# Last feed-forward of a two-layer trunk: rounded activations and their remainder as one 512-column moving operand

## The chip, the cores and the metric

One core of one Trainium2 chip runs the whole program. The metric is the device time of one execution in microseconds (us). The engines are TensorE (PE in the profile, with its weight loads as PEld), VectorE (DVE), ScalarE (ACT), GpSimd (POOL) and SyncE (SP), which here only issues loads and stores.

## The reference, cut to what matters

The trunk has two layers over 272 tokens (16 meta tokens and 256 real ones), width 1024, feed-forward width 2816. Each layer adds a feed-forward, a mixer and a second feed-forward to the residual stream. At the end a last RMSNorm is applied and the meta tokens are dropped, so the second feed-forward of the last layer is needed for the 256 real tokens alone.

```python
def swiglu(x, w_gu, w_down):
    a, b = jnp.split(x @ w_gu, 2, axis=-1)
    return (jax.nn.silu(a) * b) @ w_down

for l in range(DEPTH):
    h = h + 0.5 * swiglu(rmsnorm(h, ffn1_norm[l]), ffn1_w_gu[l], ffn1_w_down[l])
    h = h + mixer(...)
    h = h + 0.5 * swiglu(rmsnorm(h, ffn2_norm[l]), ffn2_w_gu[l], ffn2_w_down[l])
h = rmsnorm(h, final_norm)
return h[:, CHUNK:]
```

Everything is float32.

## The kernel before

Activations lie with features on the partitions and tokens along the free axis. Every product of a weight block W (128x128) with an activation block X is made in the rounded format fp32r, in which both operands are split into a rounded part and a remainder: W = w_hi + w_lo and X = xh + xl. Three matmuls add into the same PSUM bank: w_hi with xh (L706), w_hi with xl (L707) and w_lo with xh (L708). Each has its own weight load, also where two of them in a row have the same weights. `use` issues this for the 8 blocks of a "piece" of weights (128x1024), 24 matmuls in all, and then raises `piece_done`.

The weights come as a stream of pieces through a ring of four slots. For each piece SP loads `raw`; ACT rounds it to `w_hi` (`split_hi`, L274) once the piece three before the one to come has been used, and DVE forms `w_lo = raw - w_hi` (`split_lo`, L437), which raises `lo_ready`. That frees the `raw` slot and lets TensorE use the piece.

A feed-forward has 66 pieces. The first 44 are 11 iterations of four: two pieces for two gate chunks (banks 0 and 1), two for two up chunks (banks 2 and 3). In iteration `it` DVE's queue holds, in this order: the split of ring slot 0; L491, which waits for the second gate piece and writes `scl = gate * r` (r is the norm's factor per token) and so raises `gate_scaled`; the splits of slots 1 and 2; L497, which waits for the second up piece and ACT's silu and writes `gv = up * act` and so raises `up_gated`; the split of slot 3; L500 (`gv = gv * r`); L502, which waits for ACT's rounded copy `gh` (L317) and writes `gl = gv - gh`. ACT's queue holds: the rounding of slots 0 and 1, silu (L315, waits for `gate_scaled`), the rounding of slots 2 and 3, and `gh` (L317, waits for L500). Both engines work their queues strictly in this order. TensorE waits for `gate_scaled` of the iteration before ahead of a new gate, and for `up_gated` of the iteration before ahead of a new up.

The other 22 pieces are the down projection, 11 for output chunks 0 to 3 (banks 0 to 3) and 11 for chunks 4 to 7 (banks 4 to 7). Its first piece waits for the last `gate_scaled`, and its fifth block (it goes to banks 2 and 3) for the last `up_gated`. The last two pieces of each eleven close two banks each, and `update_h` (L464) adds half of them to the residual `h`. In the last feed-forward it is followed by ACT's squares for the last norm (L289) and by DVE's multiplication with the gain (L470). After the last piece TensorE sums the squares (L720 to L726), and DVE, ACT and POOL scale `h` for the stores.

In the last layer only the tokens 16 to 271 are worked on, so a matmul of the last feed-forward has 256 columns; those of the first layer have 272.

Of the kernel before, what the change touches and what calls it, by code (L numbers as in the profile page):

```python
# [25 lines left out]
F32R = mybir.dt.float32r  # L26
ALU = mybir.AluOpType
ACT = mybir.ActivationFunctionType

P = 128  # L30
# [15 lines left out]
RING = 4  # L46
# [33 lines left out]
def trunk(nc, stream, h_in, gains, gn_gains, tables, squares, h_out):  # L80
    with ExitStack() as ctx:
# [48 lines left out]
        sp = sqh[:, :, :].rearrange("p a t -> p (a t)")[:, 0:SCORES]  # L130
        sp_hi, sp_lo = (g[:, FC - 2:FC, :].rearrange("p a t -> p (a t)")[:, 0:SCORES] for g in (gh, gl))
        pa = xg[:, 0, :, :].rearrange("p a t -> p (a t)")[:, 0:SCORES]
# [16 lines left out]
        def pair(n, q0):  # L149

            return bank[:, n:n + 2, q0:T]

        def first_query(l):
# [29 lines left out]
        gate_scaled, gate_act, up_gated = sem("gate_scaled"), sem("gate_act"), sem("up_gated")  # L183
        g_val, gh_ready, g_ready = sem("g_val"), sem("gh_ready"), sem("g_ready")

        unit_evicted, swapped, rot_cos, rot_sin, rotated = sem("unit_evicted"), sem("swapped"), sem("rot_cos"), sem("rot_sin"), sem("rotated")
# [246 lines left out]
        def _(eng):  # L433
# [27 lines left out]
            def update_h(rnd, p, b, factor, q0, final=False):  # L461

                c = 2 * p
                eng.scalar_tensor_tensor(h[:, c:c + 2, q0:T], pair(b, q0), factor, h[:, c:c + 2, q0:T],  # L464
                                         ALU.mult, ALU.add).then_inc(h_new, 1)
                if final:

                    eng.wait_ge(sq_ready, rnd * PAIRS + (p + 1))
                    for k in (c, c + 1):
                        eng.tensor_scalar(h[:, k, q0:T], h[:, k, q0:T], gain[:, rnd, k:k + 1], None,  # L470
                                          ALU.mult).then_inc(scaled_out, 1)
                else:
                    eng.wait_ge(h_new, (rnd - 1) * PAIRS + (p + 1))
                    scale_h(rnd, p, q0)
                    lo_of_h(rnd, p, q0)

            def ffn(l, f):
# [6 lines left out]
                with eng.Fori(0, ITERS) as it:  # L484
                    i = fi * ITERS + it
                    for j in range(4):
                        if j == 1:

                            eng.wait_ge(r_ready, l * 3 + 2 * f + 1)
                            eng.wait_ge(piece_done, base + it * 4 + 2)  # L490
                            eng.tensor_tensor(scl[:, :, q0:T], pair(0, q0), twice(r, q0), ALU.mult).then_inc(gate_scaled, 1)  # L491
                        if j == 3:

                            eng.wait_ge(gate_act, i + 1)
                            eng.wait_ge(g_ready, i + 1)
                            eng.wait_ge(piece_done, base + it * 4 + 4)
                            eng.tensor_tensor(gv[:, :, q0:T], pair(2, q0), act[:, :, q0:T], ALU.mult).then_inc(up_gated, 1)  # L497
                        split_lo(base + it * 4 + (j + RING), (off + j) % RING)
# [197 lines left out]
        def _(pe):  # L696
            def use(n, slot, blocks, before=None):
# [11 lines left out]
                mm.then_inc(piece_done, 1)  # L709

            def k_half(src_h, src_l, half, b, q0, halves=2, c0=0):
# [27 lines left out]
            def ffn(l, f):  # L739
                fi = l * 2 + f  # L740
                off = 0 if f == 0 else FFN + MIX
                base = l * PER_LAYER + off
                q0 = first_query(l) if f else 0

                def gate(n, half, before=None):
                    use(n, (off + half) % RING, k_half(xh, xl, half, 0, q0), before)

                def up(n, half, before=None):
                    use(n, (off + 2 + half) % RING, k_half(xh, xl, half, 2, q0), before)

# [4 lines left out]
                with pe.Fori(1, ITERS) as it:  # L755
                    pe.wait_ge(gate_scaled, fi * ITERS + it)
                    gate(base + it * 4, 0)
                    gate(base + it * 4 + 1, 1)
                    pe.wait_ge(up_gated, fi * ITERS + it)
                    up(base + it * 4 + 2, 0)  # L760
                    up(base + it * 4 + 3, 1)
                pe.wait_ge(gate_scaled, fi * ITERS + ITERS)
                for q in range(QUADS):
                    for c in range(ITERS):
# [9 lines left out]
                        use(base + s, (off + s) % RING,  # L774
                            [(gh[:, k, q0:T], gl[:, k, q0:T], bank[:, 4 * q + m, q0:T], first, last)
                             for k, m, first, last in blocks],

                            {4: lambda: pe.wait_ge(up_gated, fi * ITERS + ITERS)} if q == c == 0 else None)

# [240 lines left out]
```

## Time and profile before

| | |
|---|---|
| time, median of 3 runs | 1347.0 us (1346.66 to 1347.02) |
| span of the profiled execution, first to last instruction | 1345.0 us |
| granted TensorE clock, mean over the span | 0.997 |
| TensorE busy | 1321.6 us (98%), 10440 matmuls |
| DVE busy | 845.6 us (63%) |
| ACT busy | 640.3 us (48%) |
| POOL busy | 36.2 us (3%) |
| the last feed-forward | from about 1145 us of the span to about 1333 us |

The profile shows one execution, known by its span; what lies around the span, 2.0 us, is in the runs' times and not in the trace. Times in the rows count from the first instruction. A matmul's duration in the rows holds its way through the array, so matmuls overlap in them: the rate is read from the distance between starts.

### The profile page before, as it was taken

How to read it: one execution, taken by the hardware profiler on the slowest of the kernel's cores; microseconds unless marked ns; L12 is line 12 of the kernel's file. 1: busy time of each engine (PE TensorE's matmuls, PEld its weight loads, DVE VectorE, ACT ScalarE, POOL GpSimd, SP SyncE). 2: the span in 40 equal slices, each digit the busy share in tenths (PEclk: the TensorE clock that was granted, in tenths of full speed). 3: DMA queues.
4: the chain of work that ended last, by engine and by line, in shares of the span. 5: the costliest groups of instructions: out<-in, count | busy, mean ns of one | idle time of the engine just before them, and what ended most of it. 6: DMA issues, size and time to landing. Idle time of an engine off the chain costs nothing.

```text
span 1345.0 us, 26386 instructions
## 1 busy us (share of the span) xinstructions
PE 1321.6 (98%) x10440; PEld 1295.3 (96%) x10440; DVE 845.6 (63%) x980; ACT 640.3 (48%) x812; POOL 36.2 (3%) x27
## 2 busy tenths in 40 slices
PE   6999999999999999999999999999999999999996
PEld 6999999999999999999999999999999999999996
DVE  6666557756654776665576665577556557766654
ACT  5444445444545544444444444464545455544441
POOL 1000001000000010000010000010000000100000
PEclk9999999999999999999999999999999999999998
DMA  7655555553334556556556555556543345566651
GB/s 271 193 173 175 180 176 152 178 171 116 106 110 112 169 153 193 175 174 181 174 157 187 173 175 175 180 152 179 171 126 103 117 129 177 184 186 187 185 190 61
DMA packets 61205, 219.53 MB, mean 163 GB/s; under 512 B 6992, under 2 KB 8272, under 8 KB 61008
## 3 DMA queue, kind: packets, MB, share of 16 engines
q1 hardware_dynamic: 60704, 217.93, 53.4%
q8 instruction: 55, 0.90, 0.3%
q10 hardware_dynamic: 432, 0.59, 0.1%
q14 instruction: 14, 0.11, 0.0%
HBM read 217.44 MB, written 1.05 MB: 162 GB/s over the span
## 4 chain that ended last, share of the span: by engine, by line
PE 92%; DVE 4%; issue 2%; ACT 1%; DMA 0%; POOL 0%; DVEq 0%; ACTq 0%; POOLq 0%
PE bank L706 29%; PE bank L707 28%; PE bank L708 28%; PE bank L908 1%; PE bank L894 1%; PE bank L922 1%; PE bank L873 1%; DVE w_lo L437 1%; PE bank L802 1%; ACT act L346 1%; PE bank L785 1%; DVE act L533 0%; DVE r L459 0%; DMA gain<-gains 0%; DVE xg L445 0%
## 5 line engine op out<-in xcount | busy, mean ns | idle before, releaser
L437 DVE TENSOR_TENSOR w_lo<-raw,w_hi 128x1024 fp32r<-128x1024 f32 x408 | 507.7, 1249 | 308.2 <-ACT w_hi L274 304.2
L706 PE MATMUL bank<-xh,w_hi 128*128 128x272 f32 (+1 forms) x2240 | 646.6, 289 | 11.7 <-DVE xl L451 11.2
L274 ACT ACTIVATE w_hi<-raw 128x1024 fp32r<-128x1024 f32 x408 | 427.9, 1056 | 457.5 <-PE bank L708 454.2
L707 PE MATMUL bank<-xl,w_hi 128*128 128x272 f32 (+1 forms) x2240 | 642.7, 287 | 0.0
L708 PE MATMUL bank<-xh,w_lo 128*128 128x272 f32 (+1 forms) x2240 | 640.5, 286 | 0.0
L706 PEld LDWEIGHTS bank<-xh,w_hi 128*128 128x128 f32 x2240 | 423.3, 189 | 14.1 <-DVE xl L451 10.5
L707 PEld LDWEIGHTS bank<-xl,w_hi 128*128 128x128 f32 x2240 | 421.9, 188 | 0.2
L708 PEld LDWEIGHTS bank<-xh,w_lo 128*128 128x128 f32 x2240 | 422.0, 188 | 0.0
L706 PE MATMUL bank<-gh,w_hi 128*128 128x272 f32 (+1 forms) x1024 | 293.1, 286 | 0.0
L707 PE MATMUL bank<-gl,w_hi 128*128 128x272 f32 (+1 forms) x1024 | 292.1, 285 | 0.0
L708 PE MATMUL bank<-gh,w_lo 128*128 128x272 f32 (+1 forms) x1024 | 291.9, 285 | 0.0
L708 PEld LDWEIGHTS bank<-gh,w_lo 128*128 128x128 f32 x1024 | 193.0, 188 | 0.0
L707 PEld LDWEIGHTS bank<-gl,w_hi 128*128 128x128 f32 x1024 | 192.9, 188 | 0.0
L706 PEld LDWEIGHTS bank<-gh,w_hi 128*128 128x128 f32 x1024 | 192.6, 188 | 0.1
L317 ACT ACTIVATE gh<-gv 128x544 f32 (+1 forms) x44 | 28.7, 653 | 92.4 <-DVE gv L500 92.4
L250 POOL TENSOR_TENSOR ssq<-ssq,sqh 128x544 f32<-128x544 f32 x20 | 33.7, 1685 | 1297.7 <-ACT sqh L289 1297.7
L502 DVE TENSOR_TENSOR gl<-gv,gh 128x544 f32 (+1 forms) x44 | 31.6, 717 | 42.3 <-ACT gh L317 42.3
L497 DVE TENSOR_TENSOR gv<-bank,act 128x544 f32<-128x544 f32 (+1 forms) x44 | 31.4, 715 | 23.2 <-PE bank L708 23.2
L280 ACT ACTIVATE xh<-xg 128x544 fp32r<-128x544 f32 (+1 forms) x24 | 15.7, 654 | 59.3 <-DVE xg L445 59.2
L491 DVE TENSOR_TENSOR scl<-bank,r 128x544 f32<-128x544 f32 (+1 forms) x44 | 31.4, 713 | 1.1
L315 ACT ACTIVATE act<-scl 128x544 f32<-128x544 f32 (+1 forms) x44 | 28.1, 638 | 7.8 <-DVE scl L491 7.8
L500 DVE TENSOR_TENSOR gv<-gv,r 128x544 f32<-128x544 f32 (+1 forms) x44 | 31.2, 710 | 0.0
(104 smaller groups left out, 622.3 us busy)
## 6 DMA issues: line engine op xcount, KB each, us to landing
raw<-stream SPq DMA_DIRECT2D x408, 512.0 KB, 3.7
table<-tables SPq DMA_DIRECT2D x1, 2000.0 KB, 9.2
out<-h SPq DMA_DIRECT2D x4, 256.0 KB, 2.7
h<-tokens ACTq DMA_DIRECT2D x2, 272.0 KB, 5.9
h<-tokens SPq DMA_DIRECT2D x2, 272.0 KB, 6.0
dec<-squares SPq DMA_DIRECT2D x1, 192.0 KB, 8.0
square<-squares SPq DMA_DIRECT2D x1, 128.0 KB, 7.9
gain<-gains ACTq DMA_DIRECT2D x1, 28.0 KB, 5.3
```

Source lines behind the costliest of these rows:

```text
L250: pool.tensor_tensor(ssq[:, :, :], ssq[:, :, :], sqh[:, :, :], ALU.add).then_inc(ssq_added, 1)
L274: eng.activation(w_hi[:, slot, :], raw[:, slot, :], ACT.Copy).then_inc(hi_ready, 1)
L315: eng.activation(act[:, :, q0:T], scl[:, :, q0:T], ACT.Silu).then_inc(gate_act, 1)
L317: eng.activation(gh[:, bass.ds(it * 2, 2), q0:T], gv[:, :, q0:T], ACT.Copy).then_inc(gh_ready, 1)
L437: eng.tensor_tensor(w_lo[:, slot, :], raw[:, slot, :], w_hi[:, slot, :].bitcast(F32), ALU.subtract).then_inc(lo_ready, 1)
L491: eng.tensor_tensor(scl[:, :, q0:T], pair(0, q0), twice(r, q0), ALU.mult).then_inc(gate_scaled, 1)
L497: eng.tensor_tensor(gv[:, :, q0:T], pair(2, q0), act[:, :, q0:T], ALU.mult).then_inc(up_gated, 1)
L500: eng.tensor_tensor(gv[:, :, q0:T], gv[:, :, q0:T], twice(r, q0), ALU.mult).then_inc(g_val, 1)
L502: eng.tensor_tensor(gl[:, bass.ds(it * 2, 2), q0:T], gv[:, :, q0:T], gh[:, bass.ds(it * 2, 2), q0:T].bitcast(F32), ALU.subtract).then_inc( ...
L706: pe.matmul(out, wh, hi, start=first, stop=False)
L707: pe.matmul(out, wh, lo, start=False, stop=False)
L708: mm = pe.matmul(out, wl, hi, start=False, stop=last)
```

## The change

In the last feed-forward alone, the rounded activations and their remainders are laid side by side in one tile (`x_both`, `g_both`), so that one matmul with 512 moving columns takes both past the same w_hi: columns 0 to 255 of a bank then hold the product with the rounded part and columns 256 to 511 that with the remainder. The product of w_lo with the rounded part goes to columns 0 to 255, as a matmul of 256 columns. A block has two matmuls and two weight loads in place of three and three. The two halves of a bank have to be added: for gate and up by a `tensor_reduce` over pairs 256 apart, ahead of the multiplication that was there, and for the down projection by a second `scalar_tensor_tensor` on `h`. TensorE now waits for the reduce, not for the multiplication behind it, before it reuses the banks. The other feed-forwards and the mixers keep their instructions.

```diff
-        xh = sb("xh", [P, DC, T], F32R)
-        xl = sb("xl", [P, DC, T], F32R)
-        gh = sb("gh", [P, FC, T], F32R)
-        gl = sb("gl", [P, FC, T], F32R)
+        x_both = sb("x_both", [P, DC, 2, T], F32R)
+        g_both = sb("g_both", [P, FC, 2, T], F32R)
+        xh, xl = x_both[:, :, 0, :], x_both[:, :, 1, :]
+        gh, gl = g_both[:, :, 0, :], g_both[:, :, 1, :]
...
+        def sums(n):
+            return bank[:, n:n + 2, 0:SEQ], bank[:, n:n + 2, SEQ:2 * SEQ]
+        def halves_of(n):
+            return bank[:, n:n + 2, :].rearrange("p b (i t) -> p b t i", i=2)
...
                 # update_h
+                if final:
+                    eng.scalar_tensor_tensor(h[:, c:c + 2, q0:T], sums(b)[0], factor, h[:, c:c + 2, q0:T],
+                                             ALU.mult, ALU.add).then_inc(out_added, 1)
+                    eng.wait_ge(out_added, p + 1)
+                    eng.scalar_tensor_tensor(h[:, c:c + 2, q0:T], sums(b)[1], factor, h[:, c:c + 2, q0:T],
+                                             ALU.mult, ALU.add).then_inc(h_new, 1)
...
                             # DVE, gate
+                            if last:
+                                eng.tensor_reduce(scl[:, :, q0:T], halves_of(0), mybir.AxisListType.X, ALU.add).then_inc(gate_summed, 1)
+                                eng.wait_ge(gate_summed, it + 1)
+                                eng.tensor_tensor(scl[:, :, q0:T], scl[:, :, q0:T], twice(r, q0), ALU.mult).then_inc(gate_scaled, 1)
...
                             # DVE, up
+                            if last:
+                                eng.tensor_reduce(gv[:, :, q0:T], halves_of(2), mybir.AxisListType.X, ALU.add).then_inc(up_summed, 1)
+                                eng.wait_ge(up_summed, it + 1)
+                                eng.tensor_tensor(gv[:, :, q0:T], gv[:, :, q0:T], act[:, :, q0:T], ALU.mult).then_inc(up_gated, 1)
...
+            def use_wide(n, slot, blocks, before=None):
+                pe.wait_ge(lo_ready, n + 1)
+                for b, (both, bk, first, last) in enumerate(blocks):
+                    if before and b in before:
+                        before[b]()
+                    wh = w_hi[:, slot, b * P:(b + 1) * P]
+                    wl = w_lo[:, slot, b * P:(b + 1) * P]
+                    pe.matmul(bank[:, bk, 0:2 * SEQ], wh, both, start=first, stop=False, skip_group_check=True)
+                    mm = pe.matmul(bank[:, bk, 0:SEQ], wl, both[:, 0, :], start=False, stop=last, skip_group_check=True)
+                mm.then_inc(piece_done, 1)
...
+                last_ffn = first_query(l) > 0 and f == 1
+                gate_free, up_free, freed = (gate_summed, up_summed, 0) if last_ffn else (gate_scaled, up_gated, fi * ITERS)
...
-                    pe.wait_ge(gate_scaled, fi * ITERS + it)
+                    pe.wait_ge(gate_free, freed + it)
...
-                    pe.wait_ge(up_gated, fi * ITERS + it)
+                    pe.wait_ge(up_free, freed + it)
...
-                pe.wait_ge(gate_scaled, fi * ITERS + ITERS)
+                pe.wait_ge(gate_free, freed + ITERS)
...
+                        before = {4: lambda: pe.wait_ge(up_free, freed + ITERS)} if q == c == 0 else None
```

## Rows read from the trace of the kernel before

**Rows 1.** Page, part 1: busy time and share of the span.

```profile
PE 1321.6 (98%) x10440; PEld 1295.3 (96%) x10440; DVE 845.6 (63%) x980; ACT 640.3 (48%) x812; POOL 36.2 (3%) x27
```

**Rows 2.** Windows; the last feed-forward in steady state (busy us, count, clock, DMA).

```profile
1180.25:1270.00 89.75, 89.75 (x770) 89.75 (x769) 59.89 (x64) 42.30 (x48) 0.00 (x0) 1.00 0.63 186
```

**Rows 3.** Timeline of DVE: iteration 0, then two splits of slot 0 later.

```profile
1155.71 1.23 DVE L437 TENSOR_TENSOR w_lo<-raw,w_hi 128x1024 fp32r<-128x1024 f32 x1 [0.62 <-ACT w_hi L274]
1156.85 0.68 DVE L491 TENSOR_TENSOR scl<-bank,r 128x512 f32<-128x512 f32 x1
1157.45 1.22 DVE L437 TENSOR_TENSOR w_lo<-raw,w_hi 128x1024 fp32r<-128x1024 f32 x1
1159.18 1.23 DVE L437 TENSOR_TENSOR w_lo<-raw,w_hi 128x1024 fp32r<-128x1024 f32 x1 [0.52 <-ACT w_hi L274]
1160.33 0.68 DVE L497 TENSOR_TENSOR gv<-bank,act 128x512 f32<-128x512 f32 x1
1160.93 1.22 DVE L437 TENSOR_TENSOR w_lo<-raw,w_hi 128x1024 fp32r<-128x1024 f32 x1
1162.06 0.69 DVE L500 TENSOR_TENSOR gv<-gv,r 128x512 f32<-128x512 f32 x1
1163.73 0.69 DVE L502 TENSOR_TENSOR gl<-gv,gh 128x512 f32 x1 [0.99 <-ACT gh L317]
1164.53 1.22 DVE L437 TENSOR_TENSOR w_lo<-raw,w_hi 128x1024 fp32r<-128x1024 f32 x1
...
1185.14 1.22 DVE L437 TENSOR_TENSOR w_lo<-raw,w_hi 128x1024 fp32r<-128x1024 f32 x1
...
1263.72 1.23 DVE L437 TENSOR_TENSOR w_lo<-raw,w_hi 128x1024 fp32r<-128x1024 f32 x1
```

**Rows 4.** Timeline of ACT in iteration 0: silu, and the roundings behind it.

```profile
1157.57 0.63 ACT L315 ACTIVATE act<-scl 128x512 f32<-128x512 f32 x1 [0.94 <-DVE scl L491]
1158.11 1.99 ACT L274 ACTIVATE w_hi<-raw 128x1024 fp32r<-128x1024 f32 x2
```

**Rows 5.** Timeline of PE: start of gate 1, and the down projection's fifth block.

```profile
1157.67 0.38 PE L706 MATMUL bank<-xh,w_hi 128*128 128x256 f32 x1 [0.37 <-DVE scl L491]
...
1271.48 0.28 PE L706 MATMUL bank<-gh,w_hi 128*128 128x256 f32 x1
```

**Rows 6.** Lines by form: the tensor_reduce that the mixer has.

```profile
L647 DVE TENSOR_REDUCE vsum<-bank 128x4 f32<-128x512 f32 x8 | 5.5, 682 | 0.0
```

**Rows 7.** Timeline of DVE, down projections: splits six pieces apart, 256 and 272 columns.

```profile
1279.85 1.22 DVE L437 TENSOR_TENSOR w_lo<-raw,w_hi 128x1024 fp32r<-128x1024 f32 x1 [1.13 <-ACT w_hi L274]
...
1296.88 1.23 DVE L437 TENSOR_TENSOR w_lo<-raw,w_hi 128x1024 fp32r<-128x1024 f32 x1 [1.61 <-ACT w_hi L274]
...
158.08 1.23 DVE L437 TENSOR_TENSOR w_lo<-raw,w_hi 128x1024 fp32r<-128x1024 f32 x1 [1.55 <-ACT w_hi L274]
...
176.05 1.22 DVE L437 TENSOR_TENSOR w_lo<-raw,w_hi 128x1024 fp32r<-128x1024 f32 x1 [1.77 <-ACT w_hi L274]
```

**Rows 8.** Timeline of PE: 416 columns with 144 behind; then that form alone.

```profile
1024.71 0.42 PE L802 MATMUL bank<-gh,square_r 128*128 128x416 f32 x2
...
L802 PE MATMUL bank<-gh,square_r 128*128 128x144 f32 x16 | 3.6, 228 | 0.0
```

**Rows 9.** Timeline of DVE at the end: the last two updates of h.

```profile
1329.82 0.69 DVE L464 SCALAR_TENSOR_TENSOR h<-bank,h 128x512 f32<-128x512 f32 x1 [6.20 <-PE bank L708]
1331.21 1.82 DVE L470 TENSOR_SCALAR h<-h,gain 128x256 f32<-128x256 f32 x2 [0.70 <-ACT sqh L289]
1332.95 0.68 DVE L464 SCALAR_TENSOR_TENSOR h<-bank,h 128x512 f32<-128x512 f32 x1
```

**Rows 10.** Windows; the end, after PE's last matmul (1335.47): clock in column 7.

```profile
1338.00:1339.00 1.00, 0.00 (x0) 0.00 (x0) 0.97 (x3) 0.00 (x0) 0.75 (x1) 0.59 0.00 0
```

**Rows 11.** Timeline of PE: the first stretch of the kernel, 272 columns.

```profile
9.38 0.43 PE L707 MATMUL bank<-xl,w_hi 128*128 128x272 f32 x1
...
13.46 0.43 PE L707 MATMUL bank<-xl,w_hi 128*128 128x272 f32 x1
```

More of the change, by code:

```diff
@@ L130, in trunk @@
         sp = sqh[:, :, :].rearrange("p a t -> p (a t)")[:, 0:SCORES]
-        sp_hi, sp_lo = (g[:, FC - 2:FC, :].rearrange("p a t -> p (a t)")[:, 0:SCORES] for g in (gh, gl))
+        sp_hi, sp_lo = (g_both[:, FC - 2 + i, :, :].rearrange("p a t -> p (a t)")[:, 0:SCORES] for i in range(2))
         pa = xg[:, 0, :, :].rearrange("p a t -> p (a t)")[:, 0:SCORES]
@@ L463, in update_h @@
                 c = 2 * p
-                eng.scalar_tensor_tensor(h[:, c:c + 2, q0:T], pair(b, q0), factor, h[:, c:c + 2, q0:T],
-                                         ALU.mult, ALU.add).then_inc(h_new, 1)
+                if final:
[4 more added lines that the diff above has]
+                                             ALU.mult, ALU.add).then_inc(h_new, 1)
+                else:
+                    eng.scalar_tensor_tensor(h[:, c:c + 2, q0:T], pair(b, q0), factor, h[:, c:c + 2, q0:T],
+                                             ALU.mult, ALU.add).then_inc(h_new, 1)
                 if final:
@@ L490, in ffn @@
                             eng.wait_ge(piece_done, base + it * 4 + 2)
[L491 removed]
+                            if last:
+                                eng.tensor_reduce(scl[:, :, q0:T], halves_of(0), mybir.AxisListType.X, ALU.add).then_inc(gate_summed, 1)
+                                eng.wait_ge(gate_summed, it + 1)
+                                eng.tensor_tensor(scl[:, :, q0:T], scl[:, :, q0:T], twice(r, q0), ALU.mult).then_inc(gate_scaled, 1)
+                            else:
+                                eng.tensor_tensor(scl[:, :, q0:T], pair(0, q0), twice(r, q0), ALU.mult).then_inc(gate_scaled, 1)
                         if j == 3:
@@ L709, in use, with wide_half @@
                 mm.then_inc(piece_done, 1)
+            def use_wide(n, slot, blocks, before=None):
[8 more added lines that the diff above has]
+                mm.then_inc(piece_done, 1)
+            def wide_half(both, half, b):
+                return [(both[:, 4 * half + k, :, N_META:T], b + m, half == 0 and k == 0, half == 1 and k == 3)
+                        for k in range(4) for m in range(2)]
             def k_half(src_h, src_l, half, b, q0, halves=2, c0=0):
@@ L773, in ffn @@
                         s = GU + q * ITERS + c
[L774 to L778, printed above, removed]
+                        before = {4: lambda: pe.wait_ge(up_free, freed + ITERS)} if q == c == 0 else None
+                        if last_ffn:
+                            use_wide(base + s, (off + s) % RING,
+                                     [(g_both[:, k, :, N_META:T], 4 * q + m, first, last) for k, m, first, last in blocks], before)
+                        else:
+                            use(base + s, (off + s) % RING,
+                                [(gh[:, k, q0:T], gl[:, k, q0:T], bank[:, 4 * q + m, q0:T], first, last)
+                                 for k, m, first, last in blocks], before)
             def turn_values(b):
```

14 lines of the change are left out of this document (11 added, 3 removed).

## The prediction

> **What bounds the kernel now.** I read the page's busy times first, then the waits of TensorE, then windows and timelines of the last feed-forward. The page says TensorE [rows 1]: it is to be seen that nothing else is near. The window over the last feed-forward shows it without a gap, at a granted clock of 1.00 (2.4 GHz), while DVE is busy 59.89 of 89.75 us and ACT 42.30 [rows 2]. So in this stretch each microsecond taken off the matmuls would come off the time, as long as DVE and ACT, which make the next weights and free the banks, can still follow. DVE is 67% busy, which looks like a third to spare. Its timeline says less, because both queues are strict and wait for each other.
>
> **How fast DVE and ACT can go by themselves.** Iteration 0 of the last feed-forward shows it by chance: DVE came to it late, from the norm's factor, so neither engine waits for TensorE there, only for each other. From its first split (1155.71) to the next iteration's (1164.53) are 8.82 us [rows 3]. The ring behind this is: split 0, L491, silu on ACT, the rounding of slot 2 behind silu (1157.57, 1158.11) [rows 4], split 2, L497, split 3, L500, the copy `gh` on ACT, the rounding of slot 0 behind it, split 0. Later the same split comes every (1263.72 - 1185.14) / 7 = 11.23 us [rows 3], which is TensorE's pace: 96 matmuls at 116.9 ns. So the ring has 2.4 us to spare per iteration, not 3.7.
>
> **What the reduces add.** A reduce of 512 elements takes 682 ns [rows 6], a TENSOR_TENSOR of 512 takes 0.68 us and one of 1024 takes 1.22 to 1.23 us [rows 3]. So DVE's price goes by elements read, and I take 1.22 us for a reduce that reads 1024 and writes 512. The multiplication behind it needs its result. Where nothing is needed, the next instruction starts 0.08 us ahead of the recorded end (1155.71 to 1156.85 for 1.22 to 1.23); where ACT needs a result it starts 0.04 us behind it (L491's end 1157.53, silu 1157.57) [rows 3, 4]. I take 1.22 + 0.04 = 1.26 us for each reduce with its wait. The multiplications stay, at the 0.68 us that both kinds of operand show (L497 from PSUM, L500 from SBUF) [rows 3]. Both reduces lie inside the ring, one ahead of silu, one ahead of L497, so the ring takes 8.82 + 2 x 1.26 = 11.34 us. Bounds: no dearer than two passes over 1024 elements (2.45 us), no cheaper than the 0.68 us of the row with as many results; I stay at the value of one read per element, since both kinds of instruction show it.
>
> **What the matmuls give.** The columns stay the same: 512 + 256 in place of three times 256. What can go is a cost per matmul or weight load. In the down projection six splits are 17.03 us apart at 256 columns and 17.97 at 272, over 144 matmuls: 118.3 and 124.8 ns [rows 7]. A line through both (0.41 ns a column) gives 224 ns for 512 columns. The nearest wide matmul has 416: it and the 144-column one behind it span 0.42 us, of which the second lasts 0.228, so they start 0.19 us apart [rows 8], or 0.46 ns a column, as the 256-column ones (118.3 / 256 = 0.46). In proportion 512 columns cost 236.5 ns, exactly two of 256: nothing is gained. I take 229, between these bounds. A block of the down projection then costs 229 + 118 = 347 ns against 355, and an iteration of gate and up 32 x (229 + 117) = 11.07 us.
>
> The Trainium skill ("TensorE: Matmul & The Clock Gate", Back-to-back issue gap) has the columns at full clock plus 2.5 ns for each matmul, 215.7 ns for 512. The 416-column row at 0.19 us, where that rule would have 0.176, doesn't bear it out; by it the down projection would end 2.3 us sooner than in the sum below, and gate and up no sooner.
>
> **The sum.** 11.07 is below 11.34, so gate and up go at the ring's pace.
> - Start: split 0 at 1155.71 as before; the first reduce starts 1.14 later and ends at 1158.07. TensorE started 0.14 us behind L491's end (1157.53, 1157.67) [rows 3, 5], so gate 1 starts at 1158.21, 0.54 later than before. Gate 2 would be reached at 1169.28 and is let go at 1158.21 + 11.34 = 1169.55: from here TensorE waits for DVE in each iteration.
> - End of gate and up: in iteration 10 split 0 starts at 1155.71 + 10 x 11.34 = 1269.11. The second reduce starts 1.14 + 1.26 + 2.33 (L491 to split 2) + 1.14 = 5.87 later and ends at 1276.20. The down projection starts at 1269.11 + 2.36 + 0.14 = 1271.61 and stands before its fifth block at 1273.00, until 1276.34: a gap of 3.3 us in TensorE. Before, that block started at 1271.48 [rows 5]. Late by 4.86 us. What queues behind DVE's reduce is the split of slot 3; it is not late, since its piece begins four blocks and two pieces later.
> - Down projection: 172 blocks are left, 7.3 ns off each: -1.26 us. The second addition of `update_h` in the first eleven lies in DVE's idle time (1.61 us in each piece [rows 7]).
> - Tail: the last two updates. DVE is the limit there: 3.13 us from the first to the second, although a piece takes 2.84 [rows 9]. Each gets one more L464, needing the first one's result: 0.68 + 0.04 = 0.72 us, twice, +1.44 us. Behind it come the squares, their sum on TensorE and the last scaling, so nothing hides it.
> - Sum: 4.86 - 1.26 + 1.44 = +5.0 us. Span 1345.0 + 5.0 = 1350.0; the runs stand 2.0 us above the span, so **1352.0 us**, 0.4% slower. Price of my least certain number: the reduce counts 22 times up to the fifth block, so 0.05 us in it are 1.1 us of time.
>
> **The rivals.**
> 1. As forecast, but the gap of 3.3 us also costs TensorE its clock. At the end of the kernel the last matmul ends at 1335.47, and the window 1338 to 1339 has a mean clock of 0.59, so it fell from 2.4 to 1.2 GHz some 2.7 us later [rows 10]. The gap is longer. At the kernel's start 18 matmuls stood (13.46 - 9.38) / 18 = 227 ns apart against 125 later [rows 7, 11]; 20 of them cost 2.0 us. Time: 1354. Against it: the end shows one case, with shorter work ahead of the fall. The Trainium skill (same page, The HAM clock gate) also has the clock fall after a stretch of idleness; the row agrees.
> 2. Faster: the reduce is cheap and the matmuls have a fixed cost. With a reduce of 0.68 us the ring takes 10.3 us and TensorE leads; with 512 columns at 224 ns an iteration takes 32 x (223 + 117) = 10.88, 3.5 us off in ten; the first gate isn't late and its four pieces give 0.3; the down projection gives 2.2; the tail costs 1.44. Time 1342.5. It decides when the ring is below 10.9, that is a reduce of 1.0 us or less. Rows 6 speak against it: 682 ns for 512 read.
> 3. No change: the ring is just short enough. At 1.09 us for a reduce the ring takes 11.06 and keeps TensorE's pace. Then iteration 10 starts at 1266.3, the second reduce ends at 1273.1 and the fifth block is late by 1.8 us; with -1.3 and +1.2, 1348.7.
> 4. The reduce reads its pairs, 256 elements apart, at a worse rate. At 2.45 us: 22 x 1.23 = 27 us more, 1379. No row has such pairs; the price of DVE's reads shows no dependence on the operand otherwise.
> 5. A moving operand in two runs with a gap is dearer than 236.5 ns. From 238 ns on TensorE leads again, (11.34 / 32) - 0.117; at 260 an iteration takes 12.1 us, and ten of them, the down projection's 176 blocks (24 ns each), the first gate and the tail add 15 us: 1362.
>
> **How the numbers follow.** Forecast with the clock kept 0.45, rival 1 0.20, rival 2 0.08, rival 3 0.14, rival 4 0.10, rival 5 0.03. The likeliest is 1352.0; its own range is 1350.3 to 1353.9 (0.06 us on the reduce, 224 to 236.5 ns on the matmul). The range must hold 8 in 10: from rival 3's 1348.5 to rival 1's with a dearer reduce, 1357. 0.2% is 2.7 us, about what a measurement of this kernel can tell from no change. Faster: rival 2, 0.08. Same: rival 3 and the lower edge of the forecast, 0.17. Slower: 0.75.
>
> **What the profile of the changed kernel would show.** The reduces at about 1.22 us; split 0 of the last feed-forward every 11.3 us with DVE never waiting for TensorE; TensorE waiting 0.2 to 0.3 us for the reduce ahead of each gate, 1.1 ahead of gate 1 and 3.3 in the first down piece; wide matmuls 229 ns ahead of the next; clock rows at that gap; the first additions of the last two updates 3.85 us apart in place of 3.13. The forecast is wrong if DVE still waits for TensorE in each iteration (rivals 2, 3), or if the reduce is not near 1.2 us.

## The result

The change made the kernel slower: 1357.28 us median of 5 runs (1356.66 to 1357.91) against 1346.89 us (1346.66 to 1347.02), ratio 1.0077, 95% interval 1.0065 to 1.0089. Forecast were 1352.0 us and a range of 1348.5 to 1357.0. The direction was right; the loss of 10.4 us is twice the 5.0 forecast, and the time lies 0.3 us outside the range.

Part 1 of the page of the changed kernel, its span being 1354.9 us; to be set beside [rows 1]:

```profile
PE 1327.8 (98%) x9912; PEld 1276.5 (94%) x9912; DVE 873.3 (64%) x1006; ACT 638.0 (47%) x812; POOL 36.2 (3%) x27
```

There are 528 matmuls fewer, as there should be, and TensorE is still at 98%. The timeline of DVE in the changed kernel, iteration 0 of the last feed-forward, beside [rows 3]:

```profile
1159.21 1.23 DVE L446 TENSOR_TENSOR w_lo<-raw,w_hi 128x1024 fp32r<-128x1024 f32 x1 [0.62 <-ACT w_hi L283]
1160.35 1.22 DVE L508 TENSOR_REDUCE scl<-bank 128x512 f32<-128x1024 f32 x1
1161.60 0.69 DVE L510 TENSOR_TENSOR scl<-scl,r 128x512 f32<-128x512 f32 x1
1162.21 1.22 DVE L446 TENSOR_TENSOR w_lo<-raw,w_hi 128x1024 fp32r<-128x1024 f32 x1
1163.94 1.23 DVE L446 TENSOR_TENSOR w_lo<-raw,w_hi 128x1024 fp32r<-128x1024 f32 x1 [0.51 <-ACT w_hi L283]
1165.09 1.22 DVE L519 TENSOR_REDUCE gv<-bank 128x512 f32<-128x1024 f32 x1
1166.34 0.69 DVE L521 TENSOR_TENSOR gv<-gv,act 128x512 f32<-128x512 f32 x1
1166.95 1.22 DVE L446 TENSOR_TENSOR w_lo<-raw,w_hi 128x1024 fp32r<-128x1024 f32 x1
1168.08 0.69 DVE L526 TENSOR_TENSOR gv<-gv,r 128x512 f32<-128x512 f32 x1
1169.83 0.69 DVE L528 TENSOR_TENSOR g_both<-gv,g_both 128x512 f32 x1 [1.06 <-ACT g_both L326]
1170.55 1.23 DVE L446 TENSOR_TENSOR w_lo<-raw,w_hi 128x1024 fp32r<-128x1024 f32 x1
...
1272.45 1.23 DVE L446 TENSOR_TENSOR w_lo<-raw,w_hi 128x1024 fp32r<-128x1024 f32 x1
```

Look at three things. A reduce takes 1.22 us and its follower starts 1.25 us after the reduce's start (forecast 1.26). From split 0 to split 0 are 11.34 us here and (1272.45 - 1159.21) / 10 = 11.32 on average, where 11.34 was forecast, and in this stretch DVE waits for ACT alone. And split 0 starts at 1159.21, 3.50 us later than before: the kernel was already late when the changed feed-forward began.

The timeline of PE in the changed kernel, around the down projection's fifth block and at the first sum of the last squares, beside [rows 5, 9]:

```profile
1276.25 0.28 PE L746 MATMUL bank<-g_both,w_lo 128*128 128x256 f32 x1
1279.60 0.50 PE L745 MATMUL bank<-g_both,w_hi 128*128 128x512 f32 x1 [3.07 <-DVE gv L519]
...
1343.26 1.22 PE L768 MATMUL bank<-sqh,square 128*128 128x256 f32 x2 [1.21 <-ACT sqh L298]
```

The same sum in the timeline of the kernel before, PE and then DVE's first instruction behind it:

```profile
1334.34 0.70 PE L725 MATMUL bank<-sqh,square 128*128 128x256 f32 x2 [0.48 <-ACT sqh L289]
...
1335.51 0.42 DVE L457 TENSOR_SCALAR ms<-bank 128x256 f32<-128x256 f32 x1 [0.57 <-PE bank L726]
```

And the changed kernel's timeline of DVE at the last two updates and behind the squares:

```profile
1337.30 0.69 DVE L474 SCALAR_TENSOR_TENSOR h<-bank,h 128x512 f32<-128x512 f32 x1 [6.07 <-PE bank L746]
...
1341.14 0.68 DVE L474 SCALAR_TENSOR_TENSOR h<-bank,h 128x512 f32<-128x512 f32 x1
...
1345.37 0.42 DVE L466 TENSOR_SCALAR ms<-bank 128x256 f32<-128x256 f32 x1 [1.52 <-PE bank L769]
```

The gap forecast at 3.3 us is there with 3.07. The two updates are 3.84 us apart (forecast 3.85). The last line of PE's is one that the prediction didn't have: the first sum of the last squares takes 1.22 us as a pair, and 0.70 before. The windows around the gap of 3.07 us and at that sum show why; the granted clock is the third figure from the end:

```profile
1272.00:1285.00 13.00, 9.93 (x57) 8.42 (x56) 10.10 (x11) 6.70 (x8) 0.00 (x0) 1.00 0.64 192
...
1342.00:1343.00 1.00, 0.05 (x1) 0.00 (x0) 0.54 (x1) 0.42 (x1) 0.00 (x0) 1.00 0.00 0
1343.00:1344.00 1.00, 0.74 (x2) 0.65 (x3) 0.62 (x2) 0.20 (x1) 0.00 (x0) 0.52 0.00 0
1344.00:1345.00 1.00, 1.00 (x4) 0.52 (x2) 0.00 (x0) 0.00 (x0) 0.00 (x0) 0.50 0.00 0
```

Around the gap it stayed at 2.4 GHz. It fell to 1.2 GHz at about 1343, within the second of two idle stretches of TensorE (0.87 us, and 1.21 us ahead of the sum) that the added steps of the tail made longer. The same trace has the clock at 1.2 GHz once more, for 3.4 us from 15.3 us on, at the very start of the kernel; there TensorE has idle time to take it up (in layout_only it is busy for 0.73 us of the two from 16 to 18), and the splits behind it are at most 0.15 us later against before than those of layout_only, which kept the clock.

The 9.9 us between the two spans (1345.0 and 1354.9) divide as follows, each term as a difference of the same distance in both traces:

| stretch | before | changed | difference | forecast |
|---|---|---|---|---|
| start to split 0 of the last feed-forward | 1155.71 | 1159.21 | +3.50 | 0 |
| split 0 to the down projection's fifth block | 115.77 | 120.39 | +4.62 | +4.86 |
| fifth block to the last update but one | 58.34 | 57.70 | -0.64 | -1.2 |
| from there to the end | 15.2 | 17.6 | +2.4 | +1.44 |

### The profile page after: what moved, and what is told of

It is laid out like the page before. It is cut to its first block, busy times and chain, and to the rows that moved or that the text cites. A ratio compares the mean times of both kernels' runs of the same rounds, so it can differ in the third digit from the quotient of the medians.

```text
span 1354.9 us, 25411 instructions
## 1 busy us (share of the span) xinstructions
PE 1327.8 (98%) x9912; PEld 1276.5 (94%) x9912; DVE 873.3 (64%) x1006; ACT 638.0 (47%) x812; POOL 36.2 (3%) x27
## 4 chain that ended last, share of the span: by engine, by line
PE 83%; DVE 8%; issue 4%; ACT 3%; DMA 0%; ACTq 0%; DVEq 0%; POOL 0%; SPq 0%; POOLq 0%
PE bank L732 24%; PE bank L733 23%; PE bank L734 23%; PE bank L745 3%; ACT w_hi L283 2%; DVE w_lo L446 2%; PE bank L746 2%; PE bank L962 1%; PE bank L948 1%; PE bank L976 1%; PE bank L927 1%; DVE gv L519 1%; DVE scl L508 1%; PE bank L856 1%; ACT act L355 1%
## 5 line engine op out<-in xcount | busy, mean ns | idle before, releaser
L732 PE MATMUL bank<-x_both,w_hi 128*128 128x272 f32 (+1 forms) x1888 | 552.2, 292 | 10.4 <-DVE x_both L460 10.2
L733 PE MATMUL bank<-x_both,w_hi 128*128 128x272 f32 (+1 forms) x1888 | 543.9, 288 | 0.0
L734 PE MATMUL bank<-x_both,w_lo 128*128 128x272 f32 (+1 forms) x1888 | 542.9, 288 | 0.0
L732 PEld LDWEIGHTS bank<-x_both,w_hi 128*128 128x128 f32 x1888 | 356.4, 189 | 12.7 <-DVE x_both L460 8.8
L733 PEld LDWEIGHTS bank<-x_both,w_hi 128*128 128x128 f32 x1888 | 357.2, 189 | 0.2
L734 PEld LDWEIGHTS bank<-x_both,w_lo 128*128 128x128 f32 x1888 | 357.2, 189 | 0.0
L732 PE MATMUL bank<-g_both,w_hi 128*128 128x272 f32 (+1 forms) x848 | 244.0, 288 | 0.0
L733 PE MATMUL bank<-g_both,w_hi 128*128 128x272 f32 (+1 forms) x848 | 243.3, 287 | 0.0
L734 PE MATMUL bank<-g_both,w_lo 128*128 128x272 f32 (+1 forms) x848 | 243.3, 287 | 0.0
L733 PEld LDWEIGHTS bank<-g_both,w_hi 128*128 128x128 f32 x848 | 160.5, 189 | 0.0
L732 PEld LDWEIGHTS bank<-g_both,w_hi 128*128 128x128 f32 x848 | 159.5, 188 | 0.1
L734 PEld LDWEIGHTS bank<-g_both,w_lo 128*128 128x128 f32 x848 | 159.5, 188 | 0.0
L745 PE MATMUL bank<-x_both,w_hi 128*128 128x512 f32 x352 | 124.8, 398 | 0.9 <-DVE scl L508 0.9
L746 PE MATMUL bank<-x_both,w_lo 128*128 128x256 f32 x352 | 98.7, 281 | 0.0
L745 PEld LDWEIGHTS bank<-x_both,w_hi 128*128 128x128 f32 x352 | 66.2, 188 | 17.6 <-issue 2.3
L746 PEld LDWEIGHTS bank<-x_both,w_lo 128*128 128x128 f32 x352 | 66.4, 189 | 0.0
```

The lines of the kernel that those rows point to most:

```text
L732: pe.matmul(out, wh, hi, start=first, stop=False)
L733: pe.matmul(out, wh, lo, start=False, stop=False)
L734: mm = pe.matmul(out, wl, hi, start=False, stop=last)
L745: pe.matmul(bank[:, bk, 0:2 * SEQ], wh, both, start=first, stop=False, skip_group_check=True)
L746: mm = pe.matmul(bank[:, bk, 0:SEQ], wl, both[:, 0, :], start=False, stop=last, skip_group_check=True)
```

## The experiments

All times are medians of interleaved runs; the kernel before, run again beside each version, had a median of 1346.7 to 1346.9 us.

**Is it the layout?** `layout_only` is the kernel before with two declarations changed and the views of them:

```diff
-        xh = sb("xh", [P, DC, T], F32R)
-        xl = sb("xl", [P, DC, T], F32R)
-        gh = sb("gh", [P, FC, T], F32R)
-        gl = sb("gl", [P, FC, T], F32R)
+        x_both = sb("x_both", [P, DC, 2, T], F32R)
+        g_both = sb("g_both", [P, FC, 2, T], F32R)
+        xh, xl = x_both[:, :, 0, :], x_both[:, :, 1, :]
+        gh, gl = g_both[:, :, 0, :], g_both[:, :, 1, :]
```

> The kernel before with only the two tiles interleaved (rounded part and remainder side by side for each chunk); every instruction is that of before. Theory: the place of the operands in SBUF sets the distance between matmuls, and the interleaving costs 0.5 ns on each of the 9800 matmuls: about +4.5 to +5 us over the whole kernel, spread evenly, 4.4 of them ahead of the last feed-forward. Rival: the slower matmuls come with the changed program, not with the addresses: within 0.5 us of before.

Measured: 1352.49 us (1351.75 to 1352.6), ratio 1.0041 (1.0027 to 1.0055). With every instruction as before, 5.6 us are lost. The timeline of DVE in layout_only, down projection of the first feed-forward, beside the last two of [rows 7]; then split 0 of the last feed-forward:

```profile
158.24 1.23 DVE L436 TENSOR_TENSOR w_lo<-raw,w_hi 128x1024 fp32r<-128x1024 f32 x1 [1.62 <-ACT w_hi L273]
...
176.32 1.23 DVE L436 TENSOR_TENSOR w_lo<-raw,w_hi 128x1024 fp32r<-128x1024 f32 x1 [1.79 <-ACT w_hi L273]
...
1159.16 1.23 DVE L436 TENSOR_TENSOR w_lo<-raw,w_hi 128x1024 fp32r<-128x1024 f32 x1 [0.62 <-ACT w_hi L273]
```

Six pieces take 18.08 us in place of 17.97, 0.8 ns a matmul, and the last feed-forward begins 3.45 us late, as in the changed kernel (3.50). The loss was expected to be spread evenly, and is not: about 2 us of it come in the last feed-forward, whose iterations of gate and up take 11.39 us here and 11.23 before. In the changed kernel that part doesn't show, since there the ring of DVE and ACT sets the pace with 11.32.

**Does the change without that layout come out as forecast?** `planar` is the change with the two parts in two halves of a tile, which are the addresses of before:

```diff
-        x_both = sb("x_both", [P, DC, 2, T], F32R)
-        g_both = sb("g_both", [P, FC, 2, T], F32R)
-        xh, xl = x_both[:, :, 0, :], x_both[:, :, 1, :]
+        x_both = sb("x_both", [P, 2, DC, T], F32R)
+        g_both = sb("g_both", [P, 2, FC, T], F32R)
+        xh, xl = x_both[:, 0, :, :], x_both[:, 1, :, :]
...
-                return [(both[:, 4 * half + k, :, N_META:T], ...
+                return [(both[:, :, 4 * half + k, N_META:T], ...
```

> The change, but with the rounded parts in one half of the tile and the remainders in the other, so that each operand has the address that it had before; the 512-column operand then takes its two runs from far apart. Theory: the 4.4 us ahead of the last feed-forward go away, the ring of DVE and ACT stays at 11.33 us an iteration, the time is 1352 to 1353 us. Rival: the slower matmuls don't come from the addresses: 1357 us.

Measured: 1354.74 us (1352.65, and four runs from 1354.19 to 1354.81), ratio 1.0058 (1.0043 to 1.0072). The profiled run is the one at 1352.65: its splits keep a distance of 0.4 to 0.5 us ahead of before from the start up to about 1130 us (the first one is as much earlier, from the first load), and split 0 of the last feed-forward is 0.45 us ahead, so the creep is gone. Against this trace, with the same instructions, the changed kernel's split 0 is 3.95 us late: that is the price of the layout up to there, and the 3.50 against before holds the earlier first load. Four runs have 1.5 to 2.2 us more at a mean clock of 0.994 to 0.995 against 0.996. `planar_again` is the same kernel, for another profile:

> planar once more, for a profile. Theory (the clock falls at the 3.1 us gap of the down projection's first piece in most executions): with four chances in five the rows behind the gap show a granted clock of 0.50 for some microseconds, matmuls of 256 columns more than 200 ns apart, and a span near 1353. If the profile has a span near 1351, the clock stays at 1.00 there.

Measured: 1353.43 us in the profiled run and 1354.87 in the other. The profile has the fall at the gap. Windows of planar_again around the gap:

```profile
1273.00:1274.00 1.00, 0.00 (x0) 0.00 (x0) 0.61 (x1) 1.00 (x2) 0.00 (x0) 1.00 0.03 12
1274.00:1275.00 1.00, 0.00 (x0) 0.00 (x0) 1.00 (x2) 0.30 (x1) 0.00 (x0) 1.00 0.87 209
...
1276.00:1277.00 1.00, 1.00 (x7) 0.86 (x7) 1.00 (x2) 0.00 (x0) 0.00 (x0) 1.00 0.94 107
1277.00:1278.00 1.00, 1.00 (x6) 0.86 (x5) 1.00 (x2) 0.00 (x0) 0.00 (x0) 0.61 0.80 319
1278.00:1279.00 1.00, 1.00 (x4) 0.88 (x4) 0.21 (x1) 0.63 (x1) 0.00 (x0) 0.50 0.67 188
```

Its timeline of PE there, at both clocks:

```profile
1275.80 0.51 PE L745 MATMUL bank<-g_both,w_hi 128*128 128x512 f32 x1 [3.05 <-DVE gv L519]
...
1276.27 0.39 PE L745 MATMUL bank<-g_both,w_hi 128*128 128x512 f32 x1
1276.49 0.28 PE L746 MATMUL bank<-g_both,w_lo 128*128 128x256 f32 x1
...
1278.01 0.63 PE L745 MATMUL bank<-g_both,w_hi 128*128 128x512 f32 x1
1278.43 0.41 PE L746 MATMUL bank<-g_both,w_lo 128*128 128x256 f32 x1
```

TensorE is idle for 3.05 us, works again for 1.4 us at full clock, and then goes on at half (0.42 us from the wide matmul to the next in place of 0.22). The same splits show the cost: against planar's own profile, planar_again is 0.15 us later up to the gap and 1.72 behind it, 1.6 us for this fall.

In the tail the two traces are the other way round. The window of planar's profile there:

```profile
1339.00:1340.00 1.00, 0.75 (x2) 0.66 (x3) 0.62 (x2) 0.20 (x1) 0.00 (x0) 0.53 0.00 0
```

Its clock fell at about 1339, as in the changed kernel, while planar_again's stood at 1.00 through its last sums. So each of these two runs paid for one fall. A run with neither takes 1352.2 (planar_filled, below); with both it would take 1352.2 + 1.6 + 0.9 = 1354.7, which is where four of the five other runs lie. This sum is an argument; no run with both falls was profiled.

`planar_filled` fills the gap with work that nobody needs:

```diff
+                def wait_up():
+                    if last_ffn:
+                        for i in range(22):
+                            pe.matmul(bank[:, 7, 0:SEQ], w_hi[:, off % RING, 0:P], x_both[:, 0, 0, N_META:T], start=True, stop=True, ...)
+                    pe.wait_ge(up_free, freed + ITERS)
```

> planar, with 22 matmuls of 256 columns into the unused bank 7 ahead of the wait in the down projection's first piece, so that TensorE works through 2.6 of the 3.1 us gap. Theory (in four of five runs of planar, at a mean clock of 0.994 in place of 0.996, the clock fell at this gap and cost 2.1 us): all five runs at 1352 to 1353 us and a clock of 0.996. Rival (the 2.1 us come from elsewhere, as the start of the loads): the runs still lie at 1352.6 and 1354.8.

Measured: 1352.16 us (1351.92 to 1353.14), ratio 1.0042 (1.0029 to 1.0056). None of five runs is near 1354.8. This is the forecast's case, the ring without the clock, and it lies 0.2 us from the number given for it. Part of that is luck. In its trace, against before, split 0 comes 0.25 us earlier, the way from there to the fifth block is 4.64 us longer (forecast 4.86), the matmuls behind it give 0.67 (forecast 1.2), and the tail takes 1.36 more (forecast 1.44): the errors cancel. `both_filled` also fills the idle times of the tail (6 and 9 matmuls into bank 3 ahead of TensorE's last two waits):

> planar_filled, with 6 matmuls into bank 3 ahead of the wait for POOL's sum and 9 ahead of the wait for the last squares, so that TensorE has no long idle time at the end either. Theory (the clock fell to 1.2 GHz between the last piece and the last sums of squares and cost 0.94 us there): 1351.2 to 1351.4, and a clock of 1.00 in the rows of L768 and L769. Rival (the clock falls there whatever TensorE does): 1352.2.

Measured: 1352.39 us (1352.17 to 1352.72). The number expected was missed: it took the fall in the tail to happen in every run. planar_filled's profile (1351.92) has no fall there; its other runs are at 1351.98 and 1352.16, and, at a lower mean clock, at 1352.82 and 1353.14, about 0.9 more. With the filling all five lie within 0.55 us, 0.2 to 0.4 above the lower ones of planar_filled. So the fall comes in some runs and the filling seems to keep it away, but it gains nothing against a run without it.

**What are TensorE's matmuls worth, and what do the additions cost?** `no_additions` is planar with the DVE instructions and waits of before, reading columns 0 to 255; the product with the remainders is left out of the result in the last feed-forward. `down_additions` puts back only the second addition of `update_h`, so that the product is left out in gate and up alone.

```diff
-                                eng.tensor_reduce(scl[:, :, q0:T], halves_of(0), mybir.AxisListType.X, ALU.add).then_inc(gate_summed, 1)
-                                eng.wait_ge(gate_summed, it + 1)
-                                eng.tensor_tensor(scl[:, :, q0:T], scl[:, :, q0:T], twice(r, q0), ALU.mult).then_inc(gate_scaled, 1)
+                                eng.tensor_tensor(scl[:, :, q0:T], sums(0)[0], twice(r, q0), ALU.mult).then_inc(gate_scaled, 1)
...
-                gate_free, up_free, freed = (gate_summed, up_summed, 0) if last_ffn else (gate_scaled, up_gated, fi * ITERS)
+                gate_free, up_free, freed = gate_scaled, up_gated, fi * ITERS
```

> As planar, but DVE uses only the columns 0 to 255 of each bank, in the instructions and with the waits of before: the product with the remainders is left out of the result. What is left of the change is TensorE's part alone. Theory: without the reduces the ring takes 8.8 us again and TensorE leads; at 232 + 117 ns a block the last feed-forward is 2 to 3 us shorter and the tail is as before: 1344 to 1345 us. Rival (the wide matmul is worth nothing, 236.5 ns): 1347. Rival (a fixed cost of 10 ns or more per matmul goes): 1341.5 or less.

> no_additions with the second scalar_tensor_tensor of update_h put back: only the gate and up reduces are missing, and with them the remainder's product in gate and up. It splits what planar_filled (1352.2) has above no_additions (1346.3). Theory: 1.4 us for two more additions in the tail and up to 0.9 us because the clock falls ahead of the last sums of squares, so 1347.8 to 1348.7; the other 3.5 to 4.4 us belong to the ring of DVE and ACT. Rival (the tail carries most of it, the ring is hidden): 1350 or more.

Measured: no_additions 1346.33 us (1345.57 to 1346.47), ratio 0.9995 (0.9986 to 1.0005): no change that can be told. down_additions 1347.14 us (1346.81 to 1348.65), ratio 1.0006 (0.9997 to 1.0015). Four of the 11 runs of down_additions lie at 1347.87 to 1348.65, three of these at a lower mean clock, as if the tail lost its clock there too; none of them was profiled. TensorE's part is worth less than expected. The timeline of DVE in no_additions gives both halves of it:

```profile
1184.77 1.23 DVE L446 TENSOR_TENSOR w_lo<-raw,w_hi 128x1024 fp32r<-128x1024 f32 x1
...
1196.05 1.23 DVE L446 TENSOR_TENSOR w_lo<-raw,w_hi 128x1024 fp32r<-128x1024 f32 x1
...
1279.82 1.22 DVE L446 TENSOR_TENSOR w_lo<-raw,w_hi 128x1024 fp32r<-128x1024 f32 x1 [1.02 <-ACT w_hi L283]
...
1296.61 1.23 DVE L446 TENSOR_TENSOR w_lo<-raw,w_hi 128x1024 fp32r<-128x1024 f32 x1 [1.58 <-ACT w_hi L283]
```

An iteration of gate and up takes 11.28 us, no less than the 11.23 of before with three matmuls a block; six down pieces take 16.79 us against 17.03, 5 ns a block. In down_additions an iteration comes to 11.20 us, from the same TensorE instructions in that stretch; what makes these 0.08 us is open. The timeline of DVE in down_additions, one iteration and the tail:

```profile
1184.74 1.23 DVE L446 TENSOR_TENSOR w_lo<-raw,w_hi 128x1024 fp32r<-128x1024 f32 x1
...
1195.95 1.23 DVE L446 TENSOR_TENSOR w_lo<-raw,w_hi 128x1024 fp32r<-128x1024 f32 x1
...
1328.42 0.69 DVE L474 SCALAR_TENSOR_TENSOR h<-bank,h 128x512 f32<-128x512 f32 x1 [6.08 <-PE bank L742]
...
1335.54 0.42 DVE L466 TENSOR_SCALAR ms<-bank 128x256 f32<-128x256 f32 x1 [0.57 <-PE bank L765]
```

And the tail in no_additions:

```profile
1329.09 0.69 DVE L474 SCALAR_TENSOR_TENSOR h<-bank,h 128x512 f32<-128x512 f32 x1 [6.08 <-PE bank L739]
...
1334.79 0.42 DVE L466 TENSOR_SCALAR ms<-bank 128x256 f32<-128x256 f32 x1 [0.57 <-PE bank L762]
```

From planar_filled (1352.2) to down_additions (1347.1) are 5.0 us: they are what the reduces cost by way of the ring. The tail's addition shows as 1.42 us in the rows (from the last update but one to L466: 5.70 us without it and 7.12 with it), of which the runs show 0.8; ten iterations at 0.08 us less would make up about the rest.

**Which property of the layout?** These are the kernel before with unused tiles between the others, and no instruction changed:

```diff
+        ahead = sb("ahead", [P, 136])            # shift_544; 64, 256, 32 floats in shift_256, shift_1024, shift_128
         xh = sb("xh", [P, DC, T], F32R)
+        between_x = sb("between_x", [P, 16])     # xl_plus_64; 32 in xl_plus_128, 64 in xl_plus_256; the same between gh and gl
         xl = sb("xl", [P, DC, T], F32R)
+        after_x = sb("after_x", [P, 48])         # xl_plus_64; 32 in xl_plus_128, none in xl_plus_256
```

`after_x` fills up to 256 bytes, so that `gh` stays where it was within 256 bytes. shift_all_544 has its unused tile ahead of `raw`, the first tile of all.

> The kernel before with an unused tile of 544 bytes per partition ahead of xh, so that all tiles behind it move by 544 bytes against the weights; no instruction changes. Theory (the matmul's distance depends on the addresses of weights and moving operand against each other): the time moves by more than 1 us in one direction. Rival (only the order or stride of the chunks matters, not where they start): within 0.5 us of before.

> The kernel before with an unused tile of 256 bytes ahead of xh. Theory (each place of the moving operands against the weights has its own price): a time of its own, different from 1346.9 and from shift_544's 1350.8 by more than 0.5 us. Rival (only multiples of half a chunk matter, or before is simply the best case): 1346.9, or never below it.

> The kernel before with an unused tile of 1024 bytes (two weight blocks) ahead of xh. Theory as for shift_256. If the price repeats with the 512 bytes of a weight block, 1346.9.

> The kernel before with the unused tile of 544 bytes ahead of everything, so that weights and moving operands move together. Theory (their distance counts): as before, 1346.9. Rival (the place of the moving operand by itself counts): as shift_544, 1350.8.

> The kernel before with an unused tile of 128 bytes ahead of xh. shift_256 and shift_1024 cost nothing and shift_544, which is 32 bytes off the multiples of 256, cost 4.0 us. If the price repeats with 128 bytes or less: 1346.8. If it repeats only with 256: another time, by more than 0.5 us.

> The kernel before with 128 unused bytes between xh and xl and between gh and gl (and 128 behind xl, so that gh stays at a multiple of 256): the remainders move by 128 bytes against weights and rounded parts. Theory (the distance of the streams within 256 bytes sets the price): not 1346.8; the sign is open. Rival (only the 32-byte part of a shift counts): 1346.8.

> The kernel before with 256 unused bytes between xh and xl and between gh and gl. xl_plus_128 cost 2.6 us, and shifts of both tiles by 256 and 1024 bytes cost nothing. Theory (the price repeats with 256 bytes): 1346.8. Rival (any other distance between the two tiles costs): 1349 or more.

> The kernel before with 64 unused bytes between xh and xl and between gh and gl. Theory: a price of its own for each distance within 256 bytes, not 1346.8; in the interleaved layout the two are 1088 bytes apart, 64 more than a multiple of 256, so up to 5.6 us more than before (1352). Rival (the interleaved layout costs by the step between chunks, not by this distance): within 1.5 us of before.

| kernel | what moved | time, us | ratio (95%) |
|---|---|---|---|
| shift_128 | xh and xl (and all behind) by 128 bytes | 1346.87 | 1.0001 (0.9991 to 1.0010) |
| shift_256 | by 256 | 1346.81 | 1.0000 (0.9991 to 1.0009) |
| shift_1024 | by 1024 | 1346.79 | 1.0000 (0.9991 to 1.0009) |
| shift_544 | by 544, 32 more than a multiple of 256 | 1350.80 | 1.0029 (1.0018 to 1.0041) |
| shift_all_544 | everything by 544, the weights too | 1346.79 | 1.0000 (0.9991 to 1.0009) |
| xl_plus_64 | the remainders by 64 against the rounded parts | 1350.55 | 1.0028 (1.0018 to 1.0039) |
| xl_plus_128 | by 128 | 1349.31 | 1.0018 (1.0009 to 1.0028) |
| xl_plus_256 | by 256 | 1346.83 | 1.0000 (0.9991 to 1.0009) |

The expectations for shift_256, and the wider one that a shift always costs, fell: 128, 256 and 1024 bytes cost nothing. What decides is where the streams lie to each other within 256 bytes, though not every such move costs: the activations 128 bytes further from the weights are free (shift_128), the remainders 128 bytes further from the rounded parts are not (xl_plus_128). The starts of the matmuls say it more sharply, and show why shift_128 is free. For the first feed-forward's gate and up from 52 to 148 us of each trace I took the distance from one start to the next, and the mean at each of the 24 places in a piece:

```
before         120 135 125 121 124 127 119 125 124 130 124 129 125 127 127 123 128 125 121 125 126 123 124 123   mean 125.00
shift_256      121 133 126 122 124 126 120 125 124 128 125 129 125 126 128 122 128 124 121 125 127 122 125 122   mean 124.98
shift_128      125 127 128 122 128 125 121 125 127 122 125 122 121 134 125 122 124 127 119 125 124 129 124 129   mean 125.00
shift_544      125 124 123 124 125 125 127 124 127 126 130 122 127 125 125 125 125 125 125 125 127 125 127 125   mean 125.28
xl_plus_64     130 127 125 125 123 124 129 125 125 127 127 121 128 122 127 129 122 126 127 126 128 122 124 125   mean 125.56
layout_only    128 127 125 123 128 125 128 126 123 126 127 128 123 128 125 125 123 124 124 126 128 123 123 127   mean 125.56
changed        128 128 125 123 128 125 127 126 123 126 127 128 123 128 125 125 123 124 124 126 128 123 122 127   mean 125.56
```

Each place has its own value, it stays when everything moves by 256 bytes, and it changes with smaller moves. The row of shift_128 is that of before turned by 12 places, to within 1 ns at each. The layout gives a reason: the chunks of `xh` are 1088 bytes apart, 64 more than a multiple of 256, and a piece goes through four chunks with six matmuls each. A move by 128 bytes puts every chunk where the second next one was within 256 bytes, so the same 24 values come in another order. By this a move by 64 bytes would be free too, and 544, 32 more than a multiple of 64, is not; 64 was not run.

The interleaved layout has the remainders 1088 bytes behind the rounded parts, 64 more than a multiple of 256, where before they were 8704, a multiple. xl_plus_64 sets that one distance and has the mean of the interleaved layout, 125.56 ns. The single places differ, and the interleaved layout also doubles the step between chunks, so this speaks for the distance and does not prove that it is all. `gh` and `gl` are 128 within 256 apart before, 192 in xl_plus_64, 0 in xl_plus_128 and 64 in the interleaved layout. The mean distances of start to start by kind of product, in ns, taken from each whole trace behind 20 us (distances over 200 ns left out):

| | `xh`, `xl`, 272 columns | `gh`, `gl`, 272 | `xh`, `xl`, 256, last feed-forward | `gh`, `gl`, 256, last feed-forward |
|---|---|---|---|---|
| before | 125.1 | 124.9 | 117.0 | 118.2 |
| shift_128 | 125.1 | 124.9 | 116.9 | 118.3 |
| shift_544 | 125.3 | 125.5 | 118.1 | 118.5 |
| xl_plus_64 | 125.5 | 125.4 | 118.5 | 117.7 |
| xl_plus_128 | 125.1 | 125.5 | 118.5 | 117.5 |
| layout_only | 125.6 | 125.5 | 118.6 | 118.8 |

The price differs between the kinds of product: the interleaved layout costs 0.5 to 0.6 ns a matmul at 272 columns, and 1.6 ns in gate and up of the last feed-forward. And before is not the best in every column. xl_plus_128 moves `gh` and `gl` from 128 to 0 within 256, and at 256 columns the down projection becomes faster, 117.5 against 118.2. Between xl_plus_64 and layout_only (3.8 us and 5.6 us lost) the distances of `gh` and `gl` make about 1.2 us of the difference by these means.

No version with the whole result beat the kernel before. TensorE's whole gain, from split 0 of the last feed-forward to the last split of down_additions, is 0.97 us, and the tail's additions alone take 1.42.

## Why the prediction was wrong, by its own steps

The step that failed is one that the prediction hardly wrote down: "Start: split 0 at 1155.71 as before", together with "The columns stay the same". It priced columns, weight loads and DVE's work, and gave the two declarations nothing. They slow the matmuls of the whole kernel, also of the five parts whose instructions don't change, by 0.5 ns on average, and the last feed-forward began 3.5 us late (layout_only 3.45, planar 0.45 early). With a kernel whose time is 10440 matmuls, 0.5 ns in each is 5 us. The trace of before had a sign of it: 117 ns in gate and up and 118.3 in the down projection, at the same 256 columns. The prediction used both numbers and did not ask; xl_plus_128, which changes the distances of both pairs, turns this into 118.5 and 117.5.

The ring was right in each number: reduce 1.22 us (1.22), ring 11.34 us (11.32), gap 3.3 us (3.07), fifth block late by 4.86 us (4.62). That this costs the time, and not only appears in a trace, is shown by down_additions against planar_filled: without the reduces 5.0 us go.

The matmul's term was mis-sized. 229 ns was taken for the wide one, 7.3 ns off a block; no_additions shows 5 ns off in the down projection and nothing in gate and up. From its starts, a wide matmul of the down projection stands 232 ns ahead of its follower as a mean of 129, nine in ten of them between 227 and 238: midway between the value taken and the upper bound, the price in proportion to columns. The Trainium skill ("TensorE: Matmul & The Clock Gate", Back-to-back issue gap) has about 216 ns for 512 columns, as the gap of a matmul by itself; single matmuls may come near it, as planar_again's row with 0.22 us, but the mean does not. In the forecast this term was -1.2 us up to the last update but one; measured were -0.64.

The tail's additions were right (3.84 us apart for 3.85), but the sum has no term for the clock, and rival 1 looked for its price only at the gap of 3.3 us. In the changed kernel's profile the gap kept its clock and the tail lost it, 0.94 us: from L768 to L466 are 2.11 us, and 1.17 before from L725 to L457. Rival 1 did come about in planar_again, in the place named, at 1.6 us. Whether the gap cost the clock in some of the changed kernel's other runs (up to 1.2 us above the profiled one) is open; one profile shows one run.

Set against the sum: 1352.0 + 3.5 (layout, less the earlier first load) + 0.9 (clock in the tail) - 0.2 (ring) + 0.6 (matmuls) = 1356.8, and the profiled run took 1356.66. It is the fastest of the five; the median lies 0.6 us above it, and nothing on record says what makes that. Rivals 2, 3 and 4 are out by the reduce's 1.22 us, rival 5 by the wide matmul's 232 ns. In rival 3 the ring at 1.09 us for a reduce comes to 11.08 us by the prediction's own terms, not 11.06; that changes nothing.

## What to carry to other kernels

A tile that is laid out anew is a change to every instruction that reads it, also where the code is the same; with thousands of like instructions, check the distance between starts ahead of the place that was changed, first of all. Spare time on two engines that wait for each other is not the idle share of either: take one round of their ring from a stretch in which the third engine doesn't hold them up, and add to that. And an addition taken off TensorE's columns, which cost almost nothing to keep apart, has to pay for itself twice: in the ring and in the tail.

## What the runs showed of the hardware

The distance between fp32r matmuls depends on where the moving operands lie against the weights (shift_544 against shift_all_544) and against each other (xl_plus_64 and xl_plus_128), within 256 bytes of a partition: 124.98 to 125.56 ns as a mean at 272 columns, 119 to 135 ns at single places, 117.0 to 118.8 ns as a mean at 256 columns in the last feed-forward. Moving everything together by 544 bytes changes nothing. What in the memory makes this is open. No layout tried was faster than the one of before as a whole, but the down projection at 256 columns was, with `gl` a multiple of 256 bytes behind `gh`. A wide fp32r matmul costs nearly in proportion to its columns: the 512-column one and its 256-column follower take about 350 ns in the down projection and 350 to 353 in gate and up, where three of 256 take 355 and 351. The granted clock fell from 2.4 to 1.2 GHz at two kinds of place: in planar_again 1.4 us after TensorE had begun to work again behind 3.05 us of idleness, and in the changed kernel and planar within an idle stretch of 1.2 us that followed one of 0.9 us. At both kinds it fell in some executions and not in others, with the same program. Once, at the start of the changed kernel, it fell 0.2 us after work had begun again behind 1.9 us of idleness.
